# A two-block transformer kernel: when keys, values and modulation slabs are computed around three attentions

## What is computed

```python
# first block, per layer: gates of the two branches
merged = (jax.nn.sigmoid(gate_attn) * (a @ w_up_attn[layer])
          + jax.nn.sigmoid(gate_hgrn) * (b @ w_up_hgrn[layer]))
# second block: modulation of both layers from one vector c
mod = jnp.einsum('bd,lde->lbe', jax.nn.silu(c), ada_w) + ada_b[:, None]
# layer 0, latent attention: 64 selected positions of 256, keys and values from a latent of rank 256
_, sel = lax.top_k(score, topk)
q_lat = jnp.einsum('bqhd,hdr->bqhr', qb, w_uk) * (A_QK_DIM ** -0.5)
return jnp.einsum('bqhr,hrd->bqhd', o_lat, w_uv)
# layer 1, differential attention
p = jax.nn.softmax(logits, axis=-1)
a = p[:, :, 0] - lam_full * p[:, :, 1]
# each layer: mixer, projection w_o, residual with gate (1 + g_t), layer norm, MLP
x = _layer_norm(DN_ALPHA * x + (1.0 + g_t) * y, ln_g[i, 0], ln_b[i, 0])
```

## Time and profile before

| what | value |
|---|---|
| median of 3 runs | 1145.67 us (1145.09 to 1146.24) |
| the profiled execution, its own time | 1146.26 us |
| its span in the trace | 1144.5 us |
| TensorE busy | 1070.6 us (94%) |
| GpSimd busy | 832.7 us (73%) |
| ScalarE busy | 549.8 us (48%) |
| VectorE busy | 485.5 us (42%) |
| mean granted TensorE clock | 0.988 of full speed |

### The profile page before, as it was taken

The page is one execution under the profiler, slowest core; times in us unless marked ns, Lnnn a source line. Parts: engine busy times, 40 slices in busy tenths (PEclk is TensorE's granted clock), DMA queues, the critical chain, the costliest instruction groups (busy, mean ns, idle before and its releaser), DMA issues.

```text
span 1144.5 us, 16781 instructions
## 1 busy us (share of the span) xinstructions
PE 1070.6 (94%) x6634; PEld 900.7 (79%) x6634; DVE 485.5 (42%) x747; ACT 549.8 (48%) x771; POOL 832.7 (73%) x685
## 2 busy tenths in 40 slices
PE   5899999999799999998899999999999699999996
PEld 5778878787588787796678888996887379989994
DVE  5646444246654443474745222006524645230015
ACT  4643557456335574544634443443445335444442
POOL 5997766879776668671057998887786157999995
PEclk9999999999899999999999999999999899999999
DMA  7647633555377336854765767964666824565750
GB/s 249 201 137 288 228 122 116 181 182 166 105 263 233 117 120 165 308 161 138 294 215 172 237 220 276 338 193 147 206 227 229 312 84 134 176 195 184 225 161 38
DMA packets 112804, 221.65 MB, mean 194 GB/s; under 512 B 14944, under 2 KB 21462, under 8 KB 112726
## 3 DMA queue, kind: packets, MB, share of 16 engines
q1 hardware_dynamic: 107552, 210.30, 55.5%
q10 hardware_dynamic: 5174, 10.28, 2.5%
HBM read 219.48 MB, written 1.07 MB: 193 GB/s over the span
## 4 chain that ended last, share of the span: by engine, by line
PE 71%; POOL 9%; DVE 9%; ACT 4%; issue 3%; DMA 2%; ACTq 0%; DVEq 0%; SPq 0%; POOLq 0%
PE lin_ps L358 12%; PE lin_ps L360 11%; PE lin_ps L359 11%; POOL wlo L1024 9%; PE tmp_ps L365 5%; PE tmp_ps L367 5%; PE tmp_ps L366 5%; PE tmp_ps L552 3%; PE tmp_ps L653 3%; PE lin_ps L365 3%; PE lin_ps L367 3%; PE lin_ps L366 3%; ACT whi L1142 2%; PE tmp_ps L422 2%; PE lin_ps L589 1%
## 5 line engine op out<-in xcount | busy, mean ns | idle before, releaser
L1024 POOL TENSOR_TENSOR wlo<-ring,whi 128x512 fp32r<-128x512 f32 (+2 forms) x608 | 795.0, 1338 | 256.6 <-ACT whi L1142 246.8
L1142 ACT CAST whi<-ring 128x1024 fp32r<-128x1024 f32 (+2 forms) x304 | 312.6, 1034 | 412.0 <-PE lin_ps L360 224.8
L358 PE MATMUL lin_ps<-whi,hThi 128*128 128x512 f32 (+2 forms) x528 | 208.5, 395 | 13.7 <-POOL wlo L1024 8.3
L359 PE MATMUL lin_ps<-wlo,hThi 128*128 128x512 f32 (+2 forms) x528 | 201.9, 382 | 0.0
L360 PE MATMUL lin_ps<-whi,hTlo 128*128 128x512 f32 (+2 forms) x528 | 201.6, 382 | 0.0
L365 PE MATMUL tmp_ps<-hThi,whi 128*128 128x256 f32 x520 | 147.5, 284 | 0.1
L367 PE MATMUL tmp_ps<-hThi,wlo 128*128 128x256 f32 x520 | 147.1, 283 | 0.0
L366 PE MATMUL tmp_ps<-hTlo,whi 128*128 128x256 f32 x520 | 147.1, 283 | 0.0
L358 PEld LDWEIGHTS lin_ps<-whi,hThi 128*128 128x128 f32 x528 | 99.9, 189 | 48.4 <-POOL wlo L1024 15.0
L360 PEld LDWEIGHTS lin_ps<-whi,hTlo 128*128 128x128 f32 x528 | 100.0, 189 | 19.7
L1938 DVE TENSOR_TENSOR arena<-tmp_ps,arena 128x1024 f32<-128x1024 f32 x16 | 19.6, 1224 | 222.4 <-ACT arena L1369 222.4
(11 more groups left out here) (288 smaller groups left out, 1471.4 us busy)
## 6 DMA issues: line engine op xcount, KB each, us to landing
ring<-in_mlp_w SPq DMA_DIRECT2D x128, 512.0 KB, 4.4
ring<-in_ada_w SPq DMA_DIRECT2D x82, 512.0 KB, 4.8
ring<-in_w_in SPq DMA_DIRECT2D x80, 512.0 KB, 4.8
ring<-in_b_w_in SPq DMA_DIRECT2D x24, 512.0 KB, 4.5
ring<-in_w_out SPq DMA_DIRECT2D x16, 512.0 KB, 3.4
arena<-in_ada_w SPq DMA_DIRECT2D x27, 256.0 KB, 5.4
ring<-in_a_w_in SPq DMA_DIRECT2D x12, 512.0 KB, 7.4
ring<-in_w_up_hgrn SPq DMA_DIRECT2D x8, 512.0 KB, 3.5
```

The lines of the kernel that those rows point to most:

```text
L358: pe.matmul(ps, xh, hi, start=first, stop=False, skip_group_check=True)
L359: pe.matmul(ps, xh, lo, start=False, stop=False, skip_group_check=True)
L1024: pool.tensor_tensor(wlo[:, n % PARTS, cut, 0:width], source[:, cut, :], whi[:, n % PARTS, cut, 0:width].bitcast(F32), ALU.subtract).then_ ...
L1142: act.copy(whi[:, n % PARTS, :, 0:width], ring[:, u % RING, 2 * h:2 * h + 2, 0:width]).then_inc(S("high_formed"), 1)
```

## The change

In the first block `gh0` goes into the other half of `lin_ps`. In the latent attention `s0q1` moves behind the transposes of `w_uk`, only `s0k0` stays ahead of the scores, and `s0v0`, `s0k1` and `s0v1` are done at steps 0, 0 and 1; the ring slot of `w_uk` is released by a matmul inside `s0k0`; the unit of `w_o` is put ahead of that of `w_uv`. In `s2` the keys go into the other half of `lin_ps`, the group of slabs begun earlier is closed at step 2, the eight slabs of steps 4 to 6 move to steps 7 and 8 and behind the first half of the output projection, and `output_turned` comes one step earlier and its second call behind those slabs.

```diff
-FIRST_STAGED = {1: (26, 3, "s0k1"), 5: (27, 0, "s0s3"), 7: (28, 1, "s0s7")}
+FIRST_STAGED = {1: (26, 3, "s0v1"), 5: (27, 0, "s0s3"), 7: (28, 1, "s0s7")}
...
-                           {0: [gates("ga1", GA0 + HALF, 4)], 1: [gates("gh0", GH0, 0), gates("gh0", GH0, 4)],
+                           {0: [gates("ga1", GA0 + HALF, 4)], 1: [gates("gh0", GH0, 0, True), gates("gh0", GH0, 4)],
...
-            def project(name, w):
-
-                ada_close()
+            def project(name, w, behind=None):
+
+                if behind is None:
+                    ada_close()
                 linear_part(f"{name}y0", w, 0, HALF, hT, 0, half=turn_lin[f"{name}o0"][0],
-                            mid=lambda: output_turned(name, 1))
+                            mid=None if behind else (lambda: output_turned(name, 1)))
+                if behind:
+                    behind()
+                    output_turned(name, 1)
                 linear_part(f"{name}y0", w, 0, HALF, hT, 4)
...
+            linear_feat("s0q1", w, HALF, hT)
+            reserve(HALF, (slice(0, HALF), win(I["a_w_o_2"][0], 0, HALF, 0)))
+
+            def keys_of(h):
+
                 ps = open_tmp(f"s0k{h}")
                 for c in range(4):
                     for r in range(2):
                         mm = pe.matmul(ps[:, c // 2, (c % 2) * T:(c % 2) * T + T],
                                        wukT[:, r, (4 * h + c) * P:(4 * h + c + 1) * P], ckvT[:, r, :],
                                        start=(r == 0), stop=(r == 1))
+                    if h == 0 and c == 2:
+                        used(mm)
                 close_tmp(mm, f"s0k{h}")
-            wait_read("s0q0", "s0q1", "s0k0", "s0k1", "s0v0", "s0v1")
+
+            wait_read("s0ckvT", "s0wuk0", "s0wuk1")
+            keys_of(0)
...
+            wait_read("s0q0", "s0q1", "s0k0")
...
-                      {10: [lambda half: output_turned("s0", 0)]}, lag=2,
-                      after={n: (lambda n=n: (ada(2), stage_first(n))) for n in ADA_QUADS})
+                      {0: [values_of(0)], 1: [values_of(1)],
+                       3: [lambda half: wait_read("s0v0", "s0v1", "s0k1")], 10: [lambda half: output_turned("s0", 0)]},
+                      lag=2, after={0: lambda: keys_of(1),
+                                    **{n: (lambda n=n: (ada(2), stage_first(n))) for n in ADA_QUADS}})
...
             def keys(half):
-                feat_units("s2k1", open_lin("s2k1", half), w, D + HALF, hT)
+                feat_units("s2k1", open_lin("s2k1", 1 - half), w, D + HALF, hT)
...
-                       6: [landed("s2v1")], 10: [lambda half: output_turned("s2", 0)]}, lag=2,
-                      after={4: lambda: (reserve(HALF, (slice(0, HALF), win(I["b_w_o_2"][0], 0, HALF, 0))), ada(4)),
-                             5: lambda: ada(2), 6: lambda: ada(2)})
-            project("s2", I["b_w_o_2"][0])
+                       6: [landed("s2v1")]}, lag=2,
+                      after={2: ada_close, 7: lambda: (reserve(HALF, (slice(0, HALF), win(I["b_w_o_2"][0], 0, HALF, 0))), ada(2)),
+                             8: lambda: ada(2), 9: lambda: output_turned("s2", 0)})
+            project("s2", I["b_w_o_2"][0], lambda: (ada(2), ada(2), ada_close()))
```

More of the change, by code:

```diff
@@ L826, in _ @@
                     close_tmp(mm, f"s0idx{i}{g}")
-            for n in range(2):
-                linear_feat(f"s0q{n}", w, n * HALF, hT)
+            linear_feat("s0q0", w, 0, hT)
             slot = take((slice(0, HALF), I["a_w_uk_2"][0].rearrange("h d r -> (h d) r").rearrange(
@@ L859, in _, with values_of, part @@
                                        start=(r == 0), stop=(r == 1))
+                    if h == 0 and c == 2:
+                        used(mm)
                 close_tmp(mm, f"s0k{h}")
-            wait_read("s0q0", "s0q1", "s0k0", "s0k1", "s0v0", "s0v1")
+            wait_read("s0ckvT", "s0wuk0", "s0wuk1")
+            keys_of(0)
+            uv = []
+            def values_of(i):
+                def part(half):
+                    if i == 0:
+                        slot = take((0, "wuv"), (1, "wuv"))
+                        uv.append(slot.rearrange("p a b -> p (a b)").rearrange("p (r n) -> p r n", r=2))
+                    ps = open_lin(f"s0v{i}", 1 - half if i else half)
+                    for c in range(2):
+                        for r in range(2):
+                            mm = pe.matmul(ps[:, c, :], ckvT[:, r, i * P:(i + 1) * P], uv[0][:, r, c * HALF:(c + 1) * HALF],
+                                           start=(r == 0), stop=(r == 1))
+                    if i == 0:
+                        mm.then_inc(S("s0v0_full"), 1)
+                        finished("s0v0", (S("s0v0_full"), 1))
+                    else:
+                        finished("s0v1", used(mm))
+                return part
+            wait_read("s0q0", "s0q1", "s0k0")
             heads = (lambda t: lambda g, j, a: t[a * HD:(a + 1) * HD, 2 * g + j, :])
@@ L1401, in _, with queries_read, values_read, keys_read @@
                     read(ins, f"s0idx{i}{g}")
-            for n in range(2):
+            def queries_read(n):
                 ps = full_lin(f"s0q{n}")
                 read(act.mul(flat(qT[:, 4 * n:4 * n + 4, :]), flat(ps), HD ** -0.5), f"s0q{n}")
+            def values_read(i):
+                ps = full_lin_of(act, f"s0v{i}")
+                read(act.copy(vv[:, i, :], flat(ps)), f"s0v{i}")
+            def keys_read(h):
+                ps = full_tmp_of(act, f"s0k{h}")
+                read(act.copy(flat(kT[:, 4 * h:4 * h + 4, :]), flat(ps)), f"s0k{h}")
+            queries_read(0)
             for r in range(2):
@@ L1407, in _ @@
                 read(act.copy(wukT[:, r, :], flat(ps)), f"s0wuk{r}")
-            for i in range(NT):
-                ps = full_lin(f"s0v{i}")
-                read(act.copy(vv[:, i, :], flat(ps)), f"s0v{i}")
-            for h in range(2):
-                ps = full_tmp(f"s0k{h}")
-                read(act.copy(flat(kT[:, 4 * h:4 * h + 4, :]), flat(ps)), f"s0k{h}")
+            queries_read(1)
+            keys_read(0)
             quads = [(i, 2 * part + g) for part in range(2) for i in range(NT) for g in range(2)]
-            attention("s0", quads, QUAD, (Pq_second, pT_second), lag=2, no_lead=tuple(range(10)))
+            attention("s0", quads, QUAD, (Pq_second, pT_second),
+                      evacuate={0: lambda: values_read(0), 1: lambda: keys_read(1), 2: lambda: values_read(1)},
+                      lag=2, no_lead=tuple(range(10)))
             for h in range(2):
@@ L2091, in _ @@
             heads_scaled(1)
+            ada()
+            ada()
             ada_close()
```

27 lines of the change are left out of this document (7 added, 20 removed).

## The result

| | before | after |
|---|---|---|
| median of the comparison's runs | 1145.95 us | 1154.09 us |
| ratio, 95% interval | | 1.0077 [1.0062, 1.0092] |
| the profiled execution, its own time | 1146.26 us | 1157.65 us |
| its span | 1144.5 us | 1155.6 us |
| mean granted TensorE clock | 0.988 | 0.979 |

The change is slower by 8.8 us by the ratio, 8.1 us by the medians. I had forecast 1.6 us faster, with a range up to 1149.5 us: the sign was wrong, and the time lies outside. Measured a second time, beside other kernels, the ratio was 1.0090 [1.0068, 1.0112].

What follows compares the result with a forecast made beforehand. TensorE, busy 94% of the span, was taken as the bound, so its waits and half clock count. -1.7 + 3.6 - 3.5 = -1.6 us against 1146.26 gave 1144.7, for the median 1144.1 us, range 1139.0 to 1149.5.

Steps and rivals of the forecast that it cites:

- First block, -1.7 us: Attention of both layers: 0.25 us won at one TensorE wait, 0.60 us at another, 0.85 us per layer.
- Latent attention, the wait for `w_uv`, 3.45 us: Ahead of the first values: TensorE idle from 526.65 until `w_uv` lands at 530.1, its load held by `w_uk`'s slot.
- no queueing: Latent attention, lower bound: `w_uv` lands at 528.3, making the step -0.7 us; TensorE's wait under 2 us.
- rival C: Latent attention: `w_uv` lands late, its packets served together with two slabs' behind it; +3.1 us, 1148.8 us; chance 0.16.
- Latent attention, the clock, 2.0 us: Behind the wait for `w_uv`: 4 us of matmuls at half clock, 2.0 us lost, between 0 and 3.
- Latent attention, the slabs of step 3, 0.5 us: Two slabs issued behind the staged slab: 3 MB in 7.9 us from about 541; 0.5 us charged, between 0 and 1.
- Second attention, the waits, -10.2 + 8.0: Old TensorE waits of 10.2 us go; new ones of 8.0 us come at steps 5 to 7, gate rows and output.
- The five named waits: Second attention, all gone: keys' reading 1.1 us, gate rows 1.2, a slab's load 2.1, two for probabilities 5.8.
- The pace of VectorE in steps 5 to 7: Second attention, no slabs between these steps: TensorE waits about 1.7 us for VectorE three times, 5.1 us.
- The output's wait: Second attention, ahead of the output product's second half: 2.4 us for ScalarE, VectorE and three roundings of `w_o`.
- Second attention, the clock, -3.0 + 1.7: 3.0 us of lost matmul time goes with the old waits; 1.7 us of new half clock behind waits of 1.7 and 2.4.
- D: Second attention: the slabs' move gains nothing, eaten by the output's wait and VectorE's pace; +1.9 us, 1147.6 us; chance 0.10.

Runs made afterwards that it cites:

- the turn in the middle: Second attention's edit alone, with the output's second half turned in the middle of the first half product, slabs behind; against the kernel before: 1148.6 us, 1.0019.
- the mended order: Second attention's edit alone, with the output's second turn behind the first half product and ahead of slabs and closure; against the kernel before: 1143.6 us, 0.9991.
- the whole change with three mends: Whole change with `w_uk` released early, staged slab behind step 3's slabs, second turn inside the first half product; against the kernel before: 1146.6 us, 1.0002.

## Why the prediction was wrong, point by point

- **First block, -1.7 us.** The two waits went as forecast (1.46 to 1.2 by VectorE, 0.60 gone), but "so nothing new waits" was wrong: the wait for ScalarE ahead of the output's turn grew from 1.0 to 1.4 us, the weights' rest took 0.2, and 0.15 us of 0.85 are left in each layer. The time alone, -1.0 us, between -2.1 and -0.1, would have passed for a half-right term; that it came so near is in part luck.
- **Latent attention, the wait for `w_uv`, 3.45 us.** Right in mechanism and size: 3.8 us. That the start of the values was hit within 0.4 us is in part luck, since from the slot's release it took 6.7 us and not 6.0, and the release came 1.1 us early. Neither "no queueing" nor rival C.
- **Latent attention, the clock, 2.0 us.** The step as a mechanism was right and a third of the size: 2.3 us behind `w_uv` (5.97 less 3.70), near the charge, but also 3.1 us behind the slabs' waits, where I charged nothing: a slab, scores, transposes and products that took 1.94, 1.23, 1.97 and 1.72 us instead of 0.97, 0.72, 1.09 and 1.0. With smaller pieces it is 6.0 us in all. I had tied the half clock to one wait and not asked what my own queue estimate would do to it. The Trainium skill, TensorE: Matmul & The Clock Gate (section HAM oscillation), has each burst start cold when its load is awaited in between, in an example whose waits are about as long as the first here and longer than the other two. Here two of three load waits were followed by half clock (behind 3.8 us and behind the second slab's 1.6 us), and one was not (one slab's matmuls after 2.45 us took 1.07 us for eight).
- **Latent attention, the slabs of step 3, 0.5 us.** This step failed, and it is the one that an experiment priced by itself. I wrote "I charge 0.5 us, between 0 and 1". It is a waiting of 4.0 us and the 3.1 us of half clock behind it; moving the staged slab behind the urgent ones, alone, gave 6 us. I took 3 MB at 400 GB/s, 7.9 us, from 541 on, and the slab wanted at its end. The queue opened at 543.4, and from there TensorE wanted the pair after 6.9 us and had the second slab after 11.9. The seven DMAs ahead of that slab's last one, four of them the staged slab's, took 3.2 us to issue; the rate was 250 GB/s in the stretch from 544 to 548 us and 342 in the next; and the last DMA landed 8.6 us after its issue, with loads of later slabs around it. That the values were late is not the reason: with `w_uv` on time the wait was 5.0 us. The staged slab ahead of the urgent ones stands in that same paragraph of the prediction; I priced its bytes, and neither the issuing nor the 14.9 us in front of it in which SyncE issued nothing.
- **Second attention, the waits, -10.2 + 8.0.** The five named waits went. The pace of VectorE in steps 5 to 7, forecast 5.1 us, was 5.0. The output's wait was 4.5 us and not 2.4: I counted three roundings and gave them one half's time, though the third waits for a load whose slot a slab of this stretch frees only at 928.34. Not counted were 0.9 and 0.8 us for VectorE's additions of slabs and 0.8 us at the product's start. Idle time rose by 0.6 us where I had it fall by 2.2; against all seven traces of the attention left as it was, it did not change beyond their spread.
- **Second attention, the clock, -3.0 + 1.7.** Wrong sign: +2.0 us of busy time, and clear of the spread. The half clock that went with the old waits came back behind the new ones; 14 matmuls behind the 4.5 us wait alone, 0.43 us apart instead of 0.23, lost 2.8 us.
- **The rivals.** D, that the slabs' move gains nothing, was the right idea for the second attention, with the place right (the output, ScalarE's three roundings). I gave it 0.10 and no loss. No rival had both stages lose, and none was about SyncE's order, so the range ended at 1149.5.

The sum by the measured terms: -1.2 (of which the edit -0.3) + 9.65 + 2.6 = 11.1 us in the profiled execution, 8.8 us in the comparison. Against the forecast's -1.7 + 3.6 - 3.5, the latent attention's term was off by 6.0 us, the second attention's by 6.1 and the first block's by 1.4 (0.5 with the spread that came with it). So two steps failed, of like size: the slabs of step 3 at 0.5 us, and the second attention, where the output's wait came out at 4.5 us instead of 2.4 and its half clock was charged at 1.7 us and set off against 3.0.

## What to carry to other kernels

A DMA that waits for a late event holds up everything behind it on its queue: ask when the queue reopens and when the first load behind it is wanted, and price the issuing and the landing in between, not the bytes alone (here 6.9 us were left and 11.9 needed). A slot of a ring is released best by its last reader: a later matmul cost 6 us here. Charge each new wait of TensorE with the half clock that may follow, 2.3 to 3.1 us here behind waits of 3.8, 4.0 (in two) and 4.5 us. When work is put behind something to fill a wait, look for the conversion of the next operand: it must be asked for ahead of the filling work, and its loads must not depend on it. A wait that is gone gains nothing if the next one for another engine grows by as much: follow a term to an instruction that both engines need, as the first block's 0.15 us instead of 0.85 show. And before a stretch of one trace is explained, look at it in traces of kernels that leave it alone: here one stretch was steady to 0.1 us and another spread over 4.

## What was not expected of the hardware

The same wait is not always followed by the same clock. Behind the closure's 0.8 us wait the product of values took 7.1 to 7.3 us in four traces (the whole change twice, the second attention's edit alone, the turn in the middle) and 5.74 us in two (the mended order, the whole change with three mends), though the instructions just ahead of it were the same. What decides that was not tried. The spread between executions of one kernel, 1143.4 to 1149.2 us for the kernel before in one set, is as large as the effects sought, which is why the medians of small edits came with intervals of a tenth of a per cent.
